# A projection made during the first layer norm and kept in DRAM until its gate, in a kernel of two transformer-like blocks

## The chip, the cores and the metric

One core of one Trainium2 chip runs the whole program; the other cores are idle. The metric is device time in microseconds (us) for one execution. The engines are TensorE (PE in the profile, its weight loads PEld), VectorE (DVE), ScalarE (ACT), GpSimd (POOL) and SyncE (SP, which here only issues transfers). Each has its own queue of instructions and works it off in order; semaphores tie the queues together.

## The reference, cut to what matters

Two blocks work on 1024 tokens of width 1024 in fp32. The first begins with a layer norm of the input and ends with a gate that adds a projection of a second input, p (1024 tokens, 256 features):

```python
x = layer_norm(x, ln_emb_g, ln_emb_b)
z = x @ w_in[i]
xs, gs, cq, ckv, kr, gm = jnp.split(z, IN_SPLIT_POINTS, axis=-1)
ys = s5_branch(xs, ...) * jax.nn.silu(gs)
ym = mla_branch(cq, ckv, kr, cos, sin, ...) * jax.nn.silu(gm)
mix = jnp.concatenate([ys, ym], axis=-1) @ w_out[i]
u = DEEPNORM_ALPHA * x + mix
ple = jax.nn.sigmoid(u @ w_pg[i]) * (p[i] @ w_pp[i])
x = layer_norm(u + ple, ln_g[i], ln_b[i])
```

p @ w_pp depends on nothing but inputs. The second block (two attentions, gates, a feed-forward part of width 2816) is not touched by the change.

## The kernel before, in words

All activations lie transposed: features on the 128 partitions, 1024 tokens along the free dimension. SBUF is divided by hand into 50 pages of 1024 fp32 columns (`page`, `pages`), which are used again and again for other things; weights pass through a ring of four pages (`ring`), filled by SyncE in a fixed order of blocks. `B_UKV`, `B_UQ`, `B_GLU`, `B_PP`, `B_WOUT` and so on number these blocks; block b goes to ring page b % 4, once the block that was there is used. The order of the work on each engine is the order in which the program is written for it, and every dependency is a semaphore.

A code matmul with fp32 operands shows as two records in the trace. A "tile" is 128 output features by 1024 tokens, over two PSUM banks of 512 columns (`two(b)` is banks b and b+1); a "half" is one bank.

**The start.** ScalarE issues the loads of the input (`xT`, four transfers of 1 MB into `XN`), then the constants. `norm_pe`, `norm_act` and `norm_dve` share the first layer norm, called `ln_emb`:

- TensorE sums the eight feature tiles of `XN` with a matrix of ones as they land (`sum_tiles`, L738), VectorE copies the mean out of PSUM (L903), TensorE spreads it to all partitions in banks 4 to 7 (`spread_tiles`, L745, read as `SPREAD`).
- VectorE subtracts it tile by tile (L906), ScalarE squares each tile into one of two buffers (`TEMPS_1`, L880), TensorE sums the squares (L738).
- ScalarE takes the root (L882), VectorE the reciprocal (L911), TensorE spreads it (L745).
- VectorE scales each tile (L898), ScalarE applies gain and bias (L892), and TensorE begins the first of 16 tiles of z = x @ w_in (`tile`, L2616), slice by slice as the tiles become ready. ScalarE copies these tiles out (L1527).

Meanwhile SyncE has waited for the last input (`landed3`) before it loads the first blocks of weights, and GpSimd prepares columns of the second block's modulation from them (`ada_sum`, L1300 to L1306: four additions or products per block).

**The end of the attention.** After the last head (L336 turns the probabilities, L348 multiplies by the values, L317 turns the output, VectorE gates it in L365) TensorE projects p: p was loaded by GpSimd into two pages of the attention's buffers (`PT_IN`, L1356), w_pp by SyncE as ring blocks `B_PP`. Eight tiles alternate between banks 0/1 and 2/3, ScalarE copies each into `PP` (L1615) and rounds one gated head in between (L1617), VectorE makes its low part (L2216). Then comes the output projection (`split_with_ada`, `products`, L2651), which needs each weight block in a high and a low part: GpSimd's `split` makes them (L1390, L1395), one block per tile, with an `ada_sum` in between. The projection of p is used in the gate, after the second projection `w_pg`, on VectorE.

## Time and profile before

| | |
|---|---|
| time before, median of 3 runs | 2281.03 us (2280.39 to 2282.52) |
| span of the profiled execution | 2278.5 us |
| what lies between the span and the median | 2.5 us |
| TensorE busy | 2194.5 us, 96% of the span |
| VectorE, GpSimd, ScalarE busy | 1154.4, 1192.3, 754.5 us |
| DMA over the span | mean 82 GB/s |

The device time of the profiled execution is not given apart from its span; the span starts with the first instruction and ends with the last, and the median of the timed runs is 2.5 us above it. "Busy" counts instructions that compute. The chain that ended last is followed back from the last instruction: what is on it sets the time. The granted clock (PEclk) is a share of TensorE's full clock of 2.4 GHz; its lower level, 1.2 GHz, shows as 0.50.

### The profile page before, as it was taken

Reading aid. Unit: us, or ns where it says so; the run is one execution under the profiler, and the core shown is the slowest. Engines: PE = TensorE matmul, PEld = TensorE weight load, DVE = VectorE, ACT = ScalarE, POOL = GpSimd, SP = SyncE. Lnnn points to the kernel's source line nnn. Section 1 sums busy time; section 2 is a strip of 40 time slices with the busy share of each in tenths; the row PEclk is TensorE's granted clock in tenths of the full one; section 3 lists DMA queues with packets and bytes.
Section 4 is the critical chain, followed back from the end, with each engine's and each line's share of the span. In section 5 each row is a group of like instructions: output and inputs, shape, how many; then the busy total and the mean of one; then the engine's idle time right before and its main releaser. Section 6 shows DMA issues by size and latency. Waiting matters only on the chain.

```text
span 2278.5 us, 27616 instructions
## 1 busy us (share of the span) xinstructions
PE 2194.5 (96%) x10944; PEld 1609.4 (71%) x10944; DVE 1154.4 (51%) x1473; ACT 754.5 (33%) x1161; POOL 1192.3 (52%) x809
## 2 busy tenths in 40 slices
PE   6999999999999899999999999998999999999998
PEld 2454464676886687568866788876788888888886
DVE  6950844551186611550036724775966666652434
ACT  4121042332112511650036343135555555531211
POOL 2533510204787265435656765365688888844442
PEclk8999999999999999999999999999999999999999
DMA  3336232001223422101211235233122222154111
GB/s 134 111 74 104 84 85 70 4 19 47 92 84 98 143 65 84 34 10 37 89 25 51 83 111 194 87 144 130 47 62 82 83 82 84 64 182 157 47 37 74
DMA packets 62590, 187.73 MB, mean 82 GB/s; under 512 B 14903, under 2 KB 17255, under 8 KB 62415
## 3 DMA queue, kind: packets, MB, share of 16 engines
q1 hardware_dynamic: 50688, 143.30, 19.6%
q10 hardware_dynamic: 8688, 32.26, 3.8%
q0 software_dynamic: 3088, 10.43, 2.4%
q8 instruction: 87, 1.43, 0.3%
q14 instruction: 39, 0.32, 0.0%
HBM read 150.15 MB, written 33.59 MB: 81 GB/s over the span
## 4 chain that ended last, share of the span: by engine, by line
PE 89%; DVE 5%; ACT 3%; issue 2%; POOL 1%; DMA 1%; ACTq 0%; DVEq 0%
PE ps L3005 21%; PE ps L2651 16%; PE ps L2616 14%; PE ps L3124 10%; PE ps L2929 4%; PE ps L3038 3%; PE ps L325 3%; PE ps L3076 2%; PE ps L493 1%; PE ps L481 1%; PE ps L348 1%; PE ps L2731 1%; PE ps L607 1%; PE ps L618 1%; PE ps L630 1%
## 5 line engine op out<-in xcount | busy, mean ns | idle before, releaser
L1390 POOL TENSOR_TENSOR w_parts<-front,sb_zero 128x1024 fp32r<-128x1024 f32 x69 | 139.0, 2014 | 300.8 <-PE ps L3124 117.7
L3124 PE MATMUL ps<-ffn_parts,w_parts 128*128 128x512 f32 x1008 | 230.3, 389 | 1.5 <-DVE front L2577 1.5
L1463 POOL TENSOR_TENSOR up_parts<-front,up_parts 128x512 fp32r<-128x512 f32 x120 | 194.5, 1629 | 69.5 <-ACT up_parts L1736 69.5
L2616 PE MATMUL ps<-front 128*128 128x512 f32 x512 | 225.5, 599 | 2.7 <-ACT front L892 2.7
L1395 POOL TENSOR_TENSOR w_parts<-front,w_parts 128x1024 fp32r<-128x1024 f32 x75 | 207.6, 2769 | 22.5 <-ACT w_parts L1891 7.5
L3124 PEld LDWEIGHTS ps<-ffn_parts,w_parts 128*128 128x128 f32 x1008 | 189.0, 188 | 41.7 <-issue 2.6
L1300 POOL TENSOR_TENSOR front<-front,sb_csilu 128x1024 f32<-128x1024 f32 x48 | 104.3, 2172 | 210.5 <-DMA front<-w_ada 210.5
L3005 PE MATMUL ps<-t_high,up_parts 128*128 128x512 f32 x640 | 204.8, 391 | 4.9 <-ACT back L1743 4.9
L2651 PE MATMUL ps<-h_high,w_parts 128*128 128x512 f32 x672 | 187.6, 394 | 0.6 <-PE ps L2929 0.6
L2616 PEld LDWEIGHTS ps<-front 128*128 128x128 f32 x512 | 96.5, 191 | 118.6 <-issue 118.1
L3005 PE MATMUL ps<-h_high,up_parts 128*128 128x512 f32 x480 | 154.5, 389 | 1.5 <-DVE back L2345 1.5
L1983 DVE TENSOR_TENSOR back<-back 128x1024 f32<-128x1024 f32 (+11 forms) x63 | 96.3, 1529 | 97.6 <-ACT back L1559 62.0
L3005 PEld LDWEIGHTS ps<-t_high,up_parts 128*128 128x128 f32 x640 | 121.0, 189 | 30.9 <-issue 5.7
L2651 PEld LDWEIGHTS ps<-h_high,w_parts 128*128 128x128 f32 x672 | 124.0, 188 | 25.8 <-issue 1.4
L2527 DVE TENSOR_TENSOR ffn_parts<-back,ffn_parts 128x1024 fp32r<-128x1024 f32 x44 | 70.0, 1599 | 129.4 <-ACT ffn_parts L1861 129.3
L1304 POOL TENSOR_TENSOR front<-front 128x512 f32<-128x512 f32 x96 | 123.7, 1289 | 7.5
L3005 PE MATMUL ps<-t_low,up_parts 128*128 128x512 f32 x320 | 125.2, 391 | 0.0
L2345 DVE TENSOR_TENSOR back<-ps,back 128x512 f32<-128x512 f32 x78 | 53.7, 688 | 113.3 <-PE ps L3005 82.8
L3005 PEld LDWEIGHTS ps<-h_high,up_parts 128*128 128x128 f32 x480 | 90.1, 188 | 20.5 <-issue 1.9
L2651 PE MATMUL ps<-h_low,w_parts 128*128 128x512 f32 x336 | 103.8, 390 | 0.0
L1861 ACT ACTIVATE ffn_parts<-back 128x1024 fp32r<-128x1024 f32 x44 | 46.3, 1060 | 158.9 <-PE ps L3124 158.9
L2616 PE MATMUL ps<-back,front 128*128 128x512 f32 x208 | 91.1, 595 | 2.8 <-ACT back L1598 1.2
(399 smaller groups left out, 4510.6 us busy)
## 6 DMA issues: line engine op xcount, KB each, us to landing
front<-w_ada SPq DMA_DIRECT2D x48, 512.0 KB, 3.6
front<-w_up SPq DMA_DIRECT2D x44, 512.0 KB, 4.4
front<-w_down SPq DMA_DIRECT2D x22, 512.0 KB, 3.6
front<-w_in SPq DMA_DIRECT2D x16, 512.0 KB, 3.6
front<-w_out SPq DMA_DIRECT2D x16, 512.0 KB, 4.7
residual<-back ACTq DMA_DIRECT2D x2, 4096.0 KB, 15.6
front<-w_gates SPq DMA_DIRECT2D x16, 512.0 KB, 4.0
gates<-back SPq DMA_DIRECT2D x16, 512.0 KB, 3.2
```

The costliest lines, as they stand in the source:

```text
L1300: pool.tensor_tensor(rows, rows, csilu[:].unsqueeze(2).to_broadcast((P, FT, P)), ALU.mult)\
L1304: pool.tensor_tensor(x[:, 0:w], x[:, 0:w], x[:, w:2 * w], ALU.add).then_inc(S("ada_step"), 1)
L1390: pool.tensor_tensor(high, raw, zero[:, 0:1].to_broadcast((P, PAGE)), ALU.add)\
L1395: pool.tensor_tensor(low, raw, high.bitcast(F32), ALU.subtract).then_inc(S("w_split"), 1)
L1463: pool.tensor_tensor(parts[:, BANK:], src, parts[:, 0:BANK].bitcast(F32), ALU.subtract)\
L1983: link(dve.tensor_tensor(o, a, b, op))
L2527: dve.tensor_tensor(AR[4 + kk % 4], act_at(kk), AR[kk % 4].bitcast(F32), ALU.subtract)\
L2616: mm = pe.matmul(ps[:, bank + nt, :], ring[:, slot, at + k * step:at + k * step + P], rhs(k0 + k)[:, nt * BANK:(nt + 1) * BANK], start=sta ...
L2651: mm = pe.matmul(ps[:, bank + nt, :], w_[:, k * P:(k + 1) * P], x_[k][:, nt * BANK:(nt + 1) * BANK], start=k == 0 and n == 0, stop=k == FT ...
L2929: mm = pe.matmul(ps[:, 2 * j + nt, :], WR[n % 2 + w_][:, at:at + P], x_[2 * b + k][:, nt * BANK:(nt + 1) * BANK], start=b == 0 and k == 0 ...
L3005: mm = pe.matmul(o, parts[:, at + k * P:at + (k + 1) * P], x, start=p in (1, 2, 5) and k == 0 and q == 0, stop=k == 3 and q == 2, skip_gro ...
L3124: mm = pe.matmul(ps[:, 2 * m + nt, :], parts[n % 2 + w_][:, at:at + P], half_of(AR[kk % 4 + x_], nt), start=k == 0 and q == 0, stop=k == N ...
```

## The change

The projection of p is taken from its place between attention and output projection and made during the first layer norm, in 16 halves (`pp_half`); it is stored to DRAM (`projected`) and loaded back by GpSimd when the pages of `PP` are free. Its inputs are loaded by SyncE ahead of and between the parts of the layer norm's input, which SyncE now loads too; ScalarE's loads of the constants move behind its first table loads. VectorE sums six of the eight input tiles (`X_SUM`), so TensorE needs three sums for the mean in place of eight. The layer norm of the start has functions of its own (`embed_pe`, `embed_act`, `embed_dve`). With `B_PP` gone, later blocks have numbers two lower. GpSimd starts the split of the first output weights on `mla_turned` (the last probabilities turned) and not on `mla_out` (the last output).

```diff
+        PT_FIRST, W_PP, PP_FIRST, X_SUM = pages(20, 2), pages(22, 2), pages(12, FT), page(27)
+        pp_dram = nc.dram_tensor("projected", (2, P, 4, SEQ), F32, kind="Internal").ap()
...
+        PP_BANK = (4, 5, 6, 7, 0, 1, 4, 5, 0, 1, 2, 0, 1, 2, 3, 2)
+        def pp_half(pe, s):
+            m, nt = divmod(s, 2)
+            for kt in range(2):
+                at = kt * BANK + m % 4 * P
+                mm = pe.matmul(ps[:, PP_BANK[s], :], W_PP[:, m // 4, at:at + P],
+                               PT_FIRST[:, kt, nt * BANK:(nt + 1) * BANK], start=kt == 0, stop=kt == 1)
+            mm.then_inc(S("pp_tile"), 1)
+        def embed_pe(pe):
+            pe.wait_ge(S("p_landed"), 32)
+            for s in range(8):
+                if s == 6:
+                    pe.wait_ge(S("pp_read_dve"), 1)
+                pp_half(pe, s)
+            pe.wait_ge(S("x_added"), 1)
+            sum_tiles(pe, 3, ones[:], X_SUM, True, False)
+            pe.wait_ge(S("landed3"), 16)
+            sum_tiles(pe, 3, ones[:], XN[:, 6, :], False, False)
+            sum_tiles(pe, 3, ones[:], XN[:, 7, :], False, True).then_inc(S("norm_mean"), 1)
+            pe.wait_ge(S("pp_free"), 3)
+            pe.wait_ge(S("norm_stat_read"), 1)
+            spread_tiles(pe, TEMPS_1[2][:, 0:256]).then_inc(S("norm_mean_spread"), 1)
+            pe.wait_ge(S("w_pp_landed"), 16)
+            pp_half(pe, 8)
+            pp_half(pe, 9)
+            for k in range(FT):
+                if k == 2:
+                    pp_half(pe, 10)
+                pe.wait_ge(S("norm_square"), k + 1)
+                sum_tiles(pe, 3, ones[:], TEMPS_1[k % 2], k == 0, k == FT - 1).then_inc(S("norm_square_used"), 1)
+            pe.wait_ge(S("pp_free"), 4)
+            pp_half(pe, 11)
+            pe.wait_ge(S("norm_rstd"), 1)
+            spread_tiles(pe, TEMPS_1[2][:, 256:512]).then_inc(S("norm_spread"), 1)
+            pp_half(pe, 12)
+            pe.wait_ge(S("pp_free"), 5)
+            pp_half(pe, 13)
+            pe.wait_ge(S("norm_std"), 1)
+            pp_half(pe, 14)
+            pe.wait_ge(S("pp_free"), 8)
+            pp_half(pe, 15)
...
+        def embed_act(act):
...
+            for m in range(1, 4):
+                projected(2 * m, 2, m)
+            act.wait_ge(S("pp_read_dve"), 1)
+            act.wait_ge(S("pp_free"), 3)
+            act.dma_start(pp_dram[0], PP_FIRST[:, 0:4, :]).then_inc(S("pp_out0"), 16)
...
+            projected(8, 2, 4)
+            act.wait_ge(S("norm_square_used"), FT)
+            act.activation(TEMPS_1[2][:, 256:512], ps[:, 3, 0:256], ACT.Sqrt, bias=eps[:, 0:1]).then_inc(S("norm_std"), 1)
+            projected(10, 1, 5)
+            projected(11, 1, 6)
+            late = {0: 12, 2: 13, 3: 14, 5: 15}
+            for k in range(FT):
+                act.wait_ge(S("norm_scaled"), k + 1)
+                act.activation(XN[:, k, :], XN[:, k, :], ACT.Identity, scale=V("ln_emb_g", k), bias=V("ln_emb_b", k))\
+                    .then_inc(S("norm_ready"), 1)
+                if k in late:
+                    projected(late[k], 1, 0)
+            act.wait_ge(S("pp_free"), 10)
+            act.dma_start(pp_dram[1], PP_FIRST[:, 4:8, :]).then_inc(S("pp_out1"), 16)
...
+        def embed_dve(dve, link):
+            dve.wait_ge(S("pp_tile"), 2)
+            dve.tensor_copy(PP_FIRST[:, 0, :], two(4)).then_inc(S("pp_read_dve"), 1)
+            for k in range(1, 6):
+                dve.wait_ge(S(f"landed{k // 2}"), 16)
+                ins = dve.tensor_tensor(X_SUM, XN[:, 0, :] if k == 1 else X_SUM, XN[:, k, :], ALU.add)
...
+            sp.dma_start(PT_FIRST, t["pT"].rearrange("(k p) t -> p k t", p=P)).then_inc(S("p_landed"), 16)
+            sp.dma_start(W_PP[:, 0, :], t["w_pp"][0]).then_inc(S("p_landed"), 16)
+            sp.dma_start(XN[:, 0:2, :], x_in[:, 0:2, :]).then_inc(S("landed0"), 16)
+            sp.dma_start(W_PP[:, 1, :], t["w_pp"][1]).then_inc(S("w_pp_landed"), 16)
+            for h in range(1, 4):
+                sp.dma_start(XN[:, 2 * h:2 * h + 2, :], x_in[:, 2 * h:2 * h + 2, :]).then_inc(S(f"landed{h}"), 16)
             sp.wait_ge(S("landed3"), 16)
...
-            for k in range(2):
-                pool.wait_ge(S("mla_turned"), 30 + k)
-                pool.dma_start(PT_IN[k], t["pT"][k * P:(k + 1) * P, :]).then_inc(S("p_landed"), 16)
-            pool.wait_ge(S("mla_out"), 32)
+            pool.wait_ge(S("mla_turned"), 32)
...
                 split(B_WOUT + 2 * j)
+                if j == 0:
+                    pool.dma_start(PP, pp_dram.rearrange("a p k t -> p a k t")).then_inc(S("pp_back"), 16)
                 ada_sum(16 + j)
...
-            for m in range(8):
-                act.wait_ge(S("pp_tile"), m + 1)
-                act.activation(PP[:, m, :], two(2 * (m % 2)), ACT.Copy).then_inc(S("pp_free"), 1)
-                if m % 2:
-                    act.activation(MH[4 + m // 2], GM[:, m // 2, :], ACT.Copy).then_inc(S("gm_high"), 1)
+            act.wait_ge(S("mla_out"), 32)
+            for h in range(MLA_HEADS):
+                act.activation(MH[4 + h], GM[:, h, :], ACT.Copy).then_inc(S("gm_high"), 1)
...
+            dve.wait_ge(S("pp_back"), 16)
...
+            embed_pe(pe)
             pe.wait_ge(S("act_step"), ACT_STEP["c_ready"])
+            pe.wait_ge(S("pp_free"), 7)
...
-            for m in range(8):
-                block_landed(B_PP + m // 4)
-                if m == 1:
-                    pe.wait_ge(S("mla_scores_read"), 32 + MLA_HEADS)
-                elif m >= 2:
-                    pe.wait_ge(S("pp_free"), m - 1)
-                mm = tile(2 * (m % 2), (B_PP + m // 4) % RING, lambda k: PT_IN[k], kts=2,
-                          at=(m % 4) * P, step=BANK)
-                mm.then_inc(S("pp_tile"), 1)
```

The order of instructions shows the two places. On TensorE, the first layer norm, from the first matmul of the program to the last of the layer norm (L738 sums, L745 spreads, L997 is a matmul of `pp_half`; a code matmul is counted once here):

```order
-L738 MATMUL ps<-front,sb_ones 32x256 x32
+L997 MATMUL ps<-back 128x512 x16
+L738 MATMUL ps<-back,sb_ones 32x256 x4
+L738 MATMUL ps<-front,sb_ones 32x256 x8
 L745 MATMUL ps<-back,sb_pick 128x256 x4
-L738 MATMUL ps<-back,sb_ones 32x256 x32
+L997 MATMUL ps<-back 128x512 x4
+L738 MATMUL ps<-back,sb_ones 32x256 x8
+L997 MATMUL ps<-back 128x512 x2
+L738 MATMUL ps<-back,sb_ones 32x256 x24
+L997 MATMUL ps<-back 128x512 x2
 L745 MATMUL ps<-back,sb_pick 128x256 x4
```

The 32 matmuls of the mean's sums become 12, and 16 of the projection stand ahead of them; eight more (halves 8 to 11) stand among the sums of squares, and eight (halves 12 to 15) behind the last spread, ahead of the first z tile.

On GpSimd, the end of the attention. Before, two loads of p, then the first split (L1390, L1395), the additions for the modulation, the second split:

```order
L1356 DMA back<-pT 128x1024 [waits mla_turned] x2
L1390 TENSOR_TENSOR w_parts_0_57<-front,sb_zero 128x1024 [waits w_landed3,mla_out]
L1395 TENSOR_TENSOR w_parts_2_59<-front,w_parts_0_57 128x1024 [waits w_high]
L1300 TENSOR_TENSOR front<-front,sb_csilu 128x1024 [waits w_landed0]
L1304 TENSOR_TENSOR front<-front 128x512 [waits ada_step]
```

And with the change, where L1498 and L1503 are the split and L1411 begins the additions:

```order
L1498 TENSOR_TENSOR w_parts_0_57<-front,sb_zero 128x1024 [waits w_landed1,mla_turned]
L1503 TENSOR_TENSOR w_parts_2_59<-front,w_parts_0_57 128x1024 [waits w_high]
L1519 DMA back<-projected 128x2x4096
L1411 TENSOR_TENSOR front<-front,sb_csilu 128x1024 [waits w_landed2]
L1415 TENSOR_TENSOR front<-front 128x512 [waits ada_step]
```

The loads of p are gone, the first split waits for an earlier semaphore, and the load of the stored projection (4 MB) is issued between it and the additions.

## Rows read from the trace of the kernel before

**Rows 1.** The page's chain of work that ended last, shares by engine.
```profile
PE 89%; DVE 5%; ACT 3%; issue 2%; POOL 1%; DMA 1%; ACTq 0%; DVEq 0%
```

**Rows 2.** The same chain in order of time, first 120 us: start, us, what.
```profile
3.18 12.37 DMA front<-xT
...
15.59 1.87 PE ps L738 x16
...
19.27 9.15 DVE front L906 x8
...
30.76 1.76 DVE back L911
...
32.57 1.08 PE ps L745 x8
...
36.31 22.49 PE ps L2616 x48
...
58.91 13.84 PE ps L2616 x32
```

**Rows 3.** Busy time by stretch; last columns granted clock, DMA share, GB/s.
```profile
core 0: us, PE busy (x) PEld busy (x) DVE busy (x) ACT busy (x) POOL busy (x), PEclk, DMA share, GB/s
...
6.00:15.50 9.50, 4.94 (x48) 1.70 (x48) 1.31 (x8) 6.30 (x10) 0.00 (x0) 1.00 1.00 399
15.50:19.20 3.70, 3.08 (x24) 1.10 (x24) 0.43 (x1) 0.00 (x0) 0.00 (x0) 0.53 0.68 223
19.20:30.30 11.10, 6.86 (x64) 1.44 (x64) 9.14 (x8) 8.47 (x9) 8.68 (x8) 0.69 0.30 118
...
36.30:39.70 3.40, 3.39 (x4) 1.49 (x5) 3.40 (x4) 3.40 (x4) 0.00 (x0) 0.51 0.00 0
39.70:51.90 12.20, 12.20 (x30) 5.45 (x29) 10.73 (x44) 4.39 (x4) 0.00 (x0) 1.00 0.00 1
```

**Rows 4.** DMA traffic from 0 to 20 us, in 40 slices.
```profile
GB/s 0 0 0 32 89 256 82 254 377 410 393 410 402 418 410 410 434 410 442 410 418 426 402 442 410 410 393 381 406 393 161 25 25 131 197 319 410 361 418 434
```

**Rows 5.** Timeline of ScalarE at the start: start, us, engine, line, what.
```profile
1.66 2.24 ACTq L1498 DMA_DIRECT2D front<-xT  x4
...
12.74 0.20 ACT L1517 ACTIVATE sb_stat<-sb_eps 128x1 f32<-128x1 f32 x1
...
20.52 8.98 ACT L880 ACTIVATE back<-front 128x1024 f32<-128x1024 f32 x8 [7.58 <-DVE front L906]
...
34.93 9.16 ACT L892 ACTIVATE front<-front,sb_vec 128x1024 f32<-128x1024 f32 x8 [4.20 <-DVE front L898]
```

**Rows 6.** The chain that ended last, from 508 to 562 us.
```profile
512.59 3.36 PE ps L348 x30
...
517.54 13.75 PE ps L2616 x32
...
545.85 16.16 PE ps L2651 x70
```

**Rows 7.** Timeline from 516 us: GpSimd, ScalarE and VectorE.
```profile
516.03 1.89 POOL L1390 TENSOR_TENSOR w_parts<-front,sb_zero 128x1024 fp32r<-128x1024 f32 x1 [6.14 <-PE ps L348]
...
518.00 2.35 POOL L1395 TENSOR_TENSOR w_parts<-front,w_parts 128x1024 fp32r<-128x1024 f32 x1
520.30 1.90 POOL L1300 TENSOR_TENSOR front<-front,sb_csilu 128x1024 f32<-128x1024 f32 x1
...
524.43 0.46 POOL L1306 TENSOR_TENSOR front<-front 128x128 f32<-128x128 f32 x1
...
525.37 1.05 ACT L1617 ACTIVATE mix_high<-back 128x1024 fp32r<-128x1024 f32 x1
526.45 1.22 DVE L2216 TENSOR_TENSOR mix_low<-back,mix_high 128x1024 fp32r<-128x1024 f32 x1 [7.64 <-ACT mix_high L1617]
```

**Rows 8.** Timeline: GpSimd issues a 2 MB load; SyncE fills a ring slot.
```profile
339.75 0.78 POOL L1343 DMA_DIRECT2D back<-ssm_out_by_feature  x1 [11.43 <-DMA ssm_out_by_feature<-back]
...
396.48 0.33 SPq L1134 DMA_DIRECT2D front<-w_ada  x1
```

More of the change, by code:

```diff
@@ new lines, in embed_act, with projected @@
+        def embed_act(act):
+            def projected(s, n, done):
+                m, nt = divmod(s, 2)
+                act.wait_ge(S("pp_tile"), s + n)
+                act.activation(PP_FIRST[:, m, nt * BANK:(nt + n) * BANK],
+                               ps[:, PP_BANK[s]:PP_BANK[s] + n, :].rearrange("p a b -> p (a b)"),
+                               ACT.Copy).then_inc(S("pp_free"), 1)
+            for m in range(1, 4):
[4 more added lines that the diff above has]
+            for k in range(FT):
+                act.wait_ge(S("norm_centred"), k + 1)
+                if k >= 2:
+                    act.wait_ge(S("norm_square_used"), k - 1)
+                act.activation(TEMPS_1[k % 2], XN[:, k, :], ACT.Square).then_inc(S("norm_square"), 1)
+            projected(8, 2, 4)
[4 more added lines that the diff above has]
+            late = {0: 12, 2: 13, 3: 14, 5: 15}
+            for k in range(FT):
+                act.wait_ge(S("norm_scaled"), k + 1)
[5 more added lines that the diff above has]
+            act.dma_start(pp_dram[1], PP_FIRST[:, 4:8, :]).then_inc(S("pp_out1"), 16)
@@ new lines, in embed_dve @@
+        def embed_dve(dve, link):
[4 more added lines that the diff above has]
+                ins = dve.tensor_tensor(X_SUM, XN[:, 0, :] if k == 1 else X_SUM, XN[:, k, :], ALU.add)
+                if k < 5:
+                    link(ins)
+            ins.then_inc(S("x_added"), 1)
+            dve.wait_ge(S("norm_mean"), 1)
+            dve.tensor_copy(TEMPS_1[2][:, 0:256], ps[:, 3, 0:256]).then_inc(S("norm_stat_read"), 1)
+            dve.wait_ge(S("norm_mean_spread"), 1)
+            for k in range(FT):
+                dve.tensor_tensor(quarters(XN[:, k, :]), quarters(XN[:, k, :]), SPREAD, ALU.subtract)\
+                    .then_inc(S("norm_centred"), 1)
+            dve.wait_ge(S("norm_std"), 1)
+            dve.reciprocal(TEMPS_1[2][:, 256:512], TEMPS_1[2][:, 256:512]).then_inc(S("norm_rstd"), 1)
+            dve.wait_ge(S("norm_spread"), 1)
+            for k in range(FT):
+                dve.wait_ge(S("norm_centred"), k + 1)
+                dve.tensor_tensor(quarters(XN[:, k, :]), quarters(XN[:, k, :]), SPREAD, ALU.mult)\
+                    .then_inc(S("norm_scaled"), 1)
@@ L991, in program @@
         BLOCKS_WIN = 32
-        B_UKV, B_UQ, B_GLU, B_PP = 32, 33, 35, 37
-        B_WOUT = 39
+        B_UKV, B_UQ, B_GLU = 32, 33, 35
+        B_WOUT = 37
         B_WPG = B_WOUT + 16
@@ L1158, in _ @@
             loads(B_GLU, B_GLU, [tile_of(t["w_glu"], m) for m in range(2)])
-            loads(B_PP, B_PP, [tile_of(t["w_pp"], m) for m in range(2)])
             def slot_free(b):
@@ L1496, in _ @@
             act.dma_start(vec[:], t["vec"]).then_inc(S("vec_landed"), 16)
-            for h in range(4):
-                act.dma_start(XN[:, 2 * h:2 * h + 2, :], t["xT"].rearrange("(k p) t -> p k t", p=P)
-                              [:, 2 * h:2 * h + 2, :]).then_inc(S(f"landed{h}"), 16)
-            act.dma_start(ident[:], t["ident"]).then_inc(S("consts_landed"), 16)
-            act.dma_start(BC, t["ssm"][:, 3 * PAIRS:].rearrange("p (i q c) -> p i q c", i=4, q=PAIRS))\
-                .then_inc(S("consts_landed"), 16)
-            act.dma_start(dsk[0:GC, :], t["dsk"]).then_inc(S("consts_landed"), 16)
-            act.dma_start(rope_c[:], t["rope_c"]).then_inc(S("consts_landed"), 16)
             act.wait_ge(S("vec_landed"), 32)
@@ L2821, in split_with_ada @@
                         pe.wait_ge(S(free), m - 1)
+                    elif before:
+                        pe.wait_ge(S(before), 7 + m)
                     else:
-                        pe.wait_ge(S(before), 7 + m)
+                        pe.wait_ge(S("mla_scores_read"), 32 + MLA_HEADS - 1 + m)
                     products(2 * (m % 2), *w_parts_1(base + 2 * m), high, low, "w_used" if m else None,
```

24 lines of the change are left out of this document (12 added, 12 removed).

## The prediction

> **What bounds the kernel now.** I read the chain of the work that ended last first: 89% of the span is TensorE [rows 1], so an edit counts for what it takes from or adds to TensorE's path, and other engines count where TensorE waits. Then I read the chain at the two places that the change touches. At the start it is not TensorE: the input lands until 15.55, and from there copy, spread, subtraction, squares, root, reciprocal and spread pass from engine to engine until the first input-projection tile starts at 36.31 [rows 2]. In the stretches 6.0 to 15.5, 15.5 to 19.2 and 19.2 to 30.3 TensorE is busy 4.9, 3.1 and 6.9 us, most of it with short sums [rows 3]. From 36.31 on it works without a break. At 517.54 the chain shows the projection of p: 32 matmul records in 13.75 us, 32 more behind them, and the output projection starts at 545.85 [rows 6]. Nothing hides it: the chain holds TensorE alone there.
>
> **What is removed: 28.3 us.** With the 8 tiles gone, the output projection can start where they started: 545.85 - 517.54 = 28.3, if its inputs are there. The weights' parts come from GpSimd in 1.89 + 2.35 us [rows 7]. Before, it starts them at 516.03, on the last attention output; now on the last transpose of scores, and the matmuls behind that transpose start at 512.59 [rows 6]. Parts ready at 512.6 + 4.3 = 516.9, 0.6 ahead of TensorE. The first four input slices were split long before. The last four need the last head: ScalarE rounds one in 1.05, VectorE subtracts in 1.22 [rows 7]. VectorE's last gating product ends near 518.8 (it starts when the transposes before 517.54 end, and takes about as long as that subtraction), so the slices stand at 521.1, then one each 1.2. TensorE wants the fifth half a tile later: 24 of 72 records in 16.16 for 70 [rows 6] are 5.5 us, so 523.1. No wait.
>
> The second tile is where the lost cover shows. GpSimd must issue the 4 MB load of the projection, do the four additions for the modulation (520.30 to 524.89, 4.6) and split again (4.3). The issue isn't in the trace: the nearest row, half as large, took 0.78 [rows 8]; below it the floor is nothing, above it twice, 1.6. I take 1.0. So 516.9 + 1.0 + 4.6 + 4.3 = 526.8, and TensorE comes at 517.54 + 11.1 = 528.6: 1.8 to spare. The raw blocks are there: the ring slots that w_pp held are freed to w_out and w_ada, and the fourth is filled at 396.48 [rows 8]. Later tiles cost GpSimd 8.9 against TensorE's 11.1. The 4 MB load lies beside weight loads; at 0.41 MB/us it is over some 12 us after 518, and the next block is wanted at 531. VectorE wants the result 150 us later. The 8 copies from PSUM on ScalarE (1.02 each) were off the path.
>
> **What is added at the start.** Times in the new schedule are primed.
>
> First the loads. The input came at 377 to 442 GB/s once it flowed [rows 4]; I use 0.415 MB/us. Landing at 15.55 with 4.19 MB of input and 0.17 ahead puts the last byte near 13.6, so completion costs 1.9. SyncE can issue about 0.9 us earlier than ScalarE did, whose four input loads begin at 1.66 [rows 5]. Ahead of the projection lie 0.17 + 1.05 (p) + 0.52 (half of w_pp) MB: 4.2 us from 2.3, plus 1.8: TensorE starts at 8.2'. All 6.3 MB, and the constants (0.6 MB), which ScalarE now issues after its table loads (the first instruction behind them was at 12.74 [rows 5], now some 2 earlier) and which thus compete, make the last input land at about 21.0'.
>
> Then 8 halves, 32 records. A tile of 32 records costs 13.84 at the upper clock [rows 2, 3]. TensorE comes from idle, and in the same case at 36.31 the granted clock was 0.51 for 3.4 us (the 1.2 GHz level, against 1.00 at 2.4) [rows 3]; half of that is lost, 1.7. So 8.2 + 13.8 + 1.7 = 23.7', later than the input: **TensorE is what the mean waits for**, not the load. Bounds: no low stretch 22.0'; one of twice the length 25.4'. VectorE's five additions (1.22 each, like the subtraction in [rows 7]) follow the landings and end about 21.0'; its copy of tile 0 goes before them. Hidden; without the cover of TensorE's 8 halves they would cost 1.2. Three sums instead of eight remain: before, the last two took 1.87 at the low clock [rows 2]; three at the high one are 1.4 to 1.6: 25.3'. Copy and spread took 1.8, from 17.46 to 19.27 [rows 2], the spread at the low clock; at the high one it should be 0.5 less: the mean is spread at 26.6', before 19.2. **+7.4.**
>
> Variance. The first square ends 2.4 after the spread before (VectorE subtracts in 1.14 [rows 2], ScalarE squares in 1.12 [rows 5]). Now halves 8 and 9 take 3.5 first and half 10 another 1.7 before the third sum. Both square buffers wait for those sums. Followed through, the last sum ends 11.85 after the spread instead of 11.0. A 1.02 copy of tile 4 stands ahead of the root on ScalarE, partly beside the last sum: +0.5. Half 11 (1.7) fits beside root and reciprocal (the latter 1.76 [rows 2]). The spread, 1.08 before, should be 0.4 quicker at the high clock. **+0.9**: reciprocal spread at 42.0', before 33.65.
>
> Halves 12 to 15. They stand between the spread and the first z tile. 12, 13 and 14 end 5.2 after it; 15 waits until ScalarE has read 13, behind three applications of gain and bias (1.15 each [rows 5]) and one copy: 5.9, so it ends at 7.7. The first z tile starts 7.8 after the spread, before 2.7: +5.1. But before it ran its first 3.4 us at the low clock, which the halves now do away with: -1.7. Its inputs are ahead of it. **+3.4.**
>
> Sum at the start: 7.4 + 0.9 + 3.4 = 11.7. VectorE's tables are later by only 8.3, and GpSimd's and ScalarE's later work hangs on TensorE or on those tables, so everything up to 517 shifts by 11.7 and no more. The two stores of the projection go to queues that nothing waits on before the first z tile's copy, 10 us after the first store should be over.
>
> **Sum.** 28.3 - 11.7 = 16.6 us less. The profiled execution has a span of 2278.5, so 2261.9; the median of the runs is 2281.03, 2.5 above the span, and I take the difference over to it: **2264.4**.
>
> **Rivals.**
> 1. The forecast, 0.74.
> 2. A wait in front of the output projection takes the place of the matmuls. For it: GpSimd had 28.3 us of cover and has 1.8 to spare now, with an issue of unknown length. Against it: all its other durations are rows. If the split started as late as before (516.03) TensorE would wait 2.8 at the first tile; if the 4 MB issue took 5 us, 2.2 at the second. Gain 13.8: 2267.2. Chance 0.10.
> 3. The loads bound the mean. Should the two queues get 0.33 MB/us together, the input lands at 25' and the mean shifts by 1.5 to 3: 2266 to 2268. For it: DMA is at 1.00 already from 6 to 15.5 [rows 3]. Chance 0.05.
> 4. The clock falls back in the gaps of the layer norm. Before, it stood at 0.53 from 15.5 to 19.2 with TensorE busy 3.1 of 3.7 us, and at 0.69 on average until 30.3 [rows 3]. Halves 8 to 10 would then cost 5 more, 12 to 15 6, the z tile its 1.7 again: 12.7 less gain, 2277.1. Against it: those were sums on 32 columns with waits between; now dense matmuls fill the gaps. Chance 0.07, the full price; part of it lies in my range. This is also what the Trainium skill says (TensorE: Matmul & The Clock Gate, HAM oscillation): pauses between bursts send the array back to half clock. By that rule the trace agrees at 36.31.
> 5. Slower: the clock stays at the low level through the whole projection. The first 8 halves would end at 35.7', 12 later, and with rival 4's 12.7 and 2 for sums and spreads: 26.7 against 16.6, 2291. It decides from 33 us of low clock beyond the 3.4 assumed, at half a us each. Against it: at 36.31 the same kind of matmul had the full clock after 3.4. Chance 0.04.
>
> **Range and chances.** Low: no low stretch at the start (-1.7), loads 1.5 earlier, spread and sums 1 less, and some for the z tiles: 2259.5. High: a low stretch of twice the length (+1.7), a second one (+1.7), rival 2 (+2.8), rounded: 2271.5. It holds cases 1 to 3 and a little of 4, 0.87. What a measurement can tell from no change is 0.2%, 4.6 us. Faster: cases 1 to 3 and part of 4, 0.92; same: the rest of 4, 0.04; slower 0.04.
>
> **What would show it.** First projection matmul near 8.2', the 8 halves over near 23.7', after the last input landed; the mean's sums right behind them. Granted clock 1.00 from some 12' to the first z tile, which starts near 49.8' and takes 13.8. The output projection's first matmul within 1 us of the last transposes of attention, at 529'; no wait over 1 us at its second tile. Wrong would be: sums that wait for the input after the halves, clock near 0.5 around 30', GpSimd's split the last to end before the second tile, or a longer pause anywhere between 52 and 517 than before.

## The result, and the profile after

The changed kernel takes 2266.12 us (median of 4 runs, 2264.39 to 2267.58); the kernel before, on the same chip, 2280.71 (4 runs, 2278.19 to 2282.52). The ratio is 0.9936, 95% interval 0.9924 to 0.9948: 14.6 us less, where 16.6 were forecast (2264.4). The profiled execution has a span of 2262.4 us; it is the fastest of the four, 2264.39, and its span is 16.1 below that of the profile before. So times at fixed points of the two traces are compared below, and not the spans.

The page's chain by engine reads almost as before [rows 1]; it moves too little to say where the time went:

```profile
PE 89%; DVE 4%; ACT 3%; issue 2%; POOL 1%; DMA 0%; DVEq 0%; ACTq 0%; SPq 0%
```

The chain in order of time does. At the start (start, us, what), against [rows 2]:

```profile
1.25 6.15 DMA back<-w_pp
...
7.54 16.65 PE ps L997 x32
24.19 1.48 PE ps L738 x24
...
26.27 0.71 PE ps L745 x8
26.98 3.63 PE ps L997 x8
...
39.42 1.76 DVE back L1086
...
41.23 0.76 PE ps L745 x8
...
47.79 1.98 PE ps L997 x4
```

The first eight halves (L997) run from 7.54 to 24.19, and the mean's three sums (L738) stand right behind them: TensorE is what the mean waits for. The mean is spread at 26.98, the reciprocal at 41.99, and the first z tile starts at 49.77. Before, these three stood at 19.27, 33.65 and 36.31.

The halves began at the low clock. The profile's granted-clock column (the third number from the end) says 1.00 from the start:

```profile
7.50:13.30 5.80, 5.76 (x7) 2.45 (x8) 1.31 (x8) 5.02 (x9) 0.00 (x0) 1.00 1.03 412
```

But the weight loads give it away (timeline of TensorE's weight loads):

```profile
11.09 0.34 PEld L997 LDWEIGHTS ps<-back 128*128 128x128 f32 x1 [0.52 <-issue]
11.94 0.34 PEld L997 LDWEIGHTS ps<-back 128*128 128x128 f32 x1 [0.52 <-issue]
12.80 0.27 PEld L997 LDWEIGHTS ps<-back 128*128 128x128 f32 x1 [0.52 <-issue]
13.30 0.19 PEld L997 LDWEIGHTS ps<-back 128*128 128x128 f32 x1 [0.24 <-issue]
13.73 0.19 PEld L997 LDWEIGHTS ps<-back 128*128 128x128 f32 x1 [0.24 <-issue]
```

Up to 12.80 they follow each other every 0.85 us, and from 13.30 every 0.43. In the trace before, the same kind of loads stood 0.85 apart where the granted clock was 0.51 [rows 3] and 0.43 apart where it was 1.00. So this is the 1.2 GHz level for 5.7 us, then 2.4 GHz, which stays until the z tile. Half of 5.7 is lost, 2.9.

On the way to the output projection little else moved. The last transposes stood at 511.53 before and stand at 523.13 now: 11.6 later, where 11.7 were forecast. Behind them is what was not forecast (the chain again, 523 to 559 us, against [rows 6]):

```profile
523.13 1.08 PE ps L338 x8
...
524.27 1.90 POOL w_parts L1498
...
526.24 2.35 POOL w_parts L1503
528.59 0.66 POOL back L1519
...
529.27 1.92 POOL front L1411
...
531.26 1.31 POOL front L1415
...
532.64 1.61 POOL front L1415
...
534.32 1.32 POOL front L1417
535.64 2.84 POOL w_parts L1498
...
538.55 3.26 POOL w_parts L1503
541.81 0.04 issue
541.85 5.78 PE ps L2758 x24
547.63 0.12 PE ps L2736 x2
```

The chain leaves TensorE and runs over GpSimd until 541.81; the waits of TensorE in this stretch (total, times, longest) are, for the output projection:

```profile
PE ps L2758 <- DVE mix_low L2322: 0.9, 1, 0.9
PE ps L2758 <- POOL w_parts L1503: 0.6, 1, 0.6
```

GpSimd's instructions are longer than the same ones are elsewhere. The addition over 128x128 takes 1.32 here and 0.46 in [rows 7], rounding a block (the first half of its split) 2.88 against 1.89, subtracting (the second half) 3.25 against 2.35. VectorE's low parts, 1.22 in [rows 7], take 8.03 for four (VectorE's timeline, the four asked for in windows that end later and later, so that each row holds one more):

```profile
531.53 2.12 DVE L2322 TENSOR_TENSOR mix_low<-back,mix_high 128x1024 fp32r<-128x1024 f32 x1 [1.12 <-ACT mix_high L1722]
531.53 3.79 DVE L2322 TENSOR_TENSOR mix_low<-back,mix_high 128x1024 fp32r<-128x1024 f32 x2 [1.12 <-ACT mix_high L1722]
531.53 5.20 DVE L2322 TENSOR_TENSOR mix_low<-back,mix_high 128x1024 fp32r<-128x1024 f32 x3 [1.12 <-ACT mix_high L1722]
531.53 8.03 DVE L2322 TENSOR_TENSOR mix_low<-back,mix_high 128x1024 fp32r<-128x1024 f32 x4 [1.12 <-ACT mix_high L1722]
```

They end at 533.65, 535.32, 536.73 and 539.56. Set beside these the ends of GpSimd's instructions in the chain above (start plus length): 532.57, 534.25, 535.64, 538.48, 541.81. Each of VectorE's ends comes 1.07 to 1.09 after one of GpSimd's, and each of GpSimd's then 0.60, 0.32, 1.75 and 2.25 after VectorE's, which is its length without company (0.75, 0.46, 1.89, 2.35) less 0.10 to 0.15. The two engines take turns, instruction by instruction: whichever starts while the other works waits until it is done. That costs GpSimd 3.6 us and VectorE 3.4 (without company the four take 4.63, experiment 7).

It isn't any work of VectorE that does this. In the first layer norm of the same kernel GpSimd's additions run beside VectorE's subtractions, which read one operand from PSUM (`ps`), and both keep the lengths that they have alone:

```profile
27.04 9.14 DVE L1083 TENSOR_TENSOR front<-front,ps 128x1024 f32<-128x1024 f32 x8 [0.92 <-PE ps L745]
29.68 0.46 POOL L1417 TENSOR_TENSOR front<-front 128x128 f32<-128x128 f32 x1
```

The low parts read both operands from SBUF.

The two waits above, 1.5 us, and some 0.4 that the tiles lose besides, are the stall. The first column for the modulation (L2736 now, L2629 before; it stands behind 72 records of the output projection in both) is at 547.63; before at 562.46. So 14.83 are gained there: 28.3 - 11.6 = 16.7, less 1.9. From that column to the end no kernel here changes anything but what GpSimd does beside the first tiles; it took 1716.0 us before and 1714.8 now, and between 1714.8 and 1717.9 in the profiles of this document (experiment 7 apart, whose stall lies behind the column). So single spans and single times differ by up to 3 us for reasons that lie behind the change.

### The profile page after: what moved, and what is told of

The parts are those of the page before. It is cut to its first block, busy times and chain, and to the rows that moved or that the text cites. A ratio compares the mean times of both kernels' runs of the same rounds, so it can differ in the third digit from the quotient of the medians.

```text
span 2262.4 us, 27546 instructions
## 1 busy us (share of the span) xinstructions
PE 2186.6 (97%) x10904; PEld 1606.9 (71%) x10904; DVE 1163.2 (51%) x1479; ACT 753.0 (33%) x1163; POOL 1190.1 (53%) x808
## 4 chain that ended last, share of the span: by engine, by line
PE 89%; DVE 4%; ACT 3%; issue 2%; POOL 1%; DMA 0%; DVEq 0%; ACTq 0%; SPq 0%
PE ps L3100 21%; PE ps L2758 16%; PE ps L2723 13%; PE ps L3219 11%; PE ps L3024 4%; PE ps L3133 3%; PE ps L327 3%; PE ps L3171 2%; PE ps L493 1%; PE ps L481 1%; PE ps L350 1%; PE ps L997 1%; PE ps L2838 1%; PE ps L618 1%; PE ps L630 1%
## 5 line engine op out<-in xcount | busy, mean ns | idle before, releaser
L1498 POOL TENSOR_TENSOR w_parts<-front,sb_zero 128x1024 fp32r<-128x1024 f32 x69 | 140.5, 2037 | 374.5 <-PE ps L3219 117.7
L1503 POOL TENSOR_TENSOR w_parts<-front,w_parts 128x1024 fp32r<-128x1024 f32 x75 | 208.8, 2784 | 22.9 <-ACT w_parts L1996 7.5
L1411 POOL TENSOR_TENSOR front<-front,sb_csilu 128x1024 f32<-128x1024 f32 x48 | 102.7, 2140 | 216.9 <-DMA front<-w_ada 216.9
L2088 DVE TENSOR_TENSOR back<-back 128x1024 f32<-128x1024 f32 (+11 forms) x63 | 90.6, 1437 | 96.8 <-ACT back L1666 62.0
L1415 POOL TENSOR_TENSOR front<-front 128x512 f32<-128x512 f32 x96 | 117.7, 1226 | 7.5
L1848 ACT ACTIVATE back<-ps 128x512 f32<-128x512 f32 x98 | 58.6, 598 | 105.8 <-PE ps L3100 99.7
```

The costliest lines, as they stand in the source:

```text
L1411: pool.tensor_tensor(rows, rows, csilu[:].unsqueeze(2).to_broadcast((P, FT, P)), ALU.mult)\
L1415: pool.tensor_tensor(x[:, 0:w], x[:, 0:w], x[:, w:2 * w], ALU.add).then_inc(S("ada_step"), 1)
L1498: pool.tensor_tensor(high, raw, zero[:, 0:1].to_broadcast((P, PAGE)), ALU.add)\
L1503: pool.tensor_tensor(low, raw, high.bitcast(F32), ALU.subtract).then_inc(S("w_split"), 1)
L2088: link(dve.tensor_tensor(o, a, b, op))
```

## The experiments

Each experiment was timed beside the kernel before, whose medians there were 2280.16 to 2280.74 us (2280.71 for the change). A difference between an experiment and the change thus carries some tenths of a us of its own, and the column's place in the traces is given beside it.

**1. The projection taken out altogether.** The gate gets the input in place of the projection (its output isn't the reference's), the layer norm is the old one, GpSimd's early split and 4 MB load stay.

```diff
-            embed_pe(pe)
+            norm_pe(pe, "ln_emb", FT, lambda k: XN[:, k, :], ones[:], True, TEMPS_1,
+                    lambda k: pe.wait_ge(S(f"landed{k // 2}"), 16))
...
-                    pool.dma_start(PP, pp_dram.rearrange("a p k t -> p a k t")).then_inc(S("pp_back"), 16)
+                    pool.dma_start(PP, t["xT"].rearrange("(k p) t -> p k t", p=P)).then_inc(S("pp_back"), 16)
```

> The end of the change alone: the projection of p is left out everywhere (the gate gets the input in its place, loaded by the same kind of 4 MB transfer, so the output is another), the first layer norm is as before the change, the split starts early. Theory: the removed matmuls are worth 28.3 us less the waits that the trace after shows at the output projection, 26.5 us, whatever happens at the start: about 2254.2 against 2280.7, and the first z tile starts at 36.3 again. Difference to the changed kernel: the whole price of the start, 11.6. Rival: the start costs less than the traces say because later stages absorb part of it (tables on VectorE, transfers), then this kernel stands at 2256 or above.

Measured: 2254.44 us (2253.42 to 2256.52), ratio 0.9889 (0.9873 to 0.9906). The z tile starts at 35.43. VectorE's four low parts take 8.22 and the waits are 1.08 and 0.58, as with the projection. So what is added at the start costs 2266.12 - 2254.44 = 11.7 us, the forecast's number; taken each against its own kernel before it is 11.5, and at the last transposes (510.94 against 523.13) 12.2, because here the input landed 0.7 earlier than in the profile before (14.84 against 15.55), which no run explains. And the stall at the output projection comes from what lies around it there, not from the projection's new place.

**2. The mean's sums all on TensorE.** VectorE's five additions go; TensorE sums eight slices instead of three.

```diff
-            pe.wait_ge(S("x_added"), 1)
-            sum_tiles(pe, 3, ones[:], X_SUM, True, False)
+            for k in range(6):
+                pe.wait_ge(S(f"landed{k // 2}"), 16)
+                sum_tiles(pe, 3, ones[:], XN[:, k, :], k == 0, False)
```

> The changed kernel without its second part: TensorE sums all eight tiles of the input for the mean, VectorE's running sum is gone. Theory: TensorE is what the mean waits for, so five sums more of 8 records stand on the path, at 1.07 us for 16 records: 2.6 us more than the changed kernel, about 2268.7. Rival: the load binds, then the sums hide beside the landings and it costs nothing.

Measured: 2268.51 us (2267.70 to 2269.19), ratio 0.9949 (0.9932 to 0.9966). From its chain:

```profile
24.20 3.64 PE ps L738 x64
```

The sums take 3.64 instead of 1.48, the z tile starts at 51.94 instead of 49.77, and the time is 2.4 longer. TensorE binds the mean, and the running sum on VectorE is worth 2.2 to 2.4 of the gain: it is hidden on VectorE and would not be on TensorE.

**3. Warming TensorE.** Ten small matmuls of ones before p has landed.

```diff
+            for i in range(10):
+                pe.matmul(ps[:, 2, 0:P], ones[:], ones[:], start=True, stop=True)
             pe.wait_ge(S("p_landed"), 32)
```

> The changed kernel, with ten small matmuls of the ones matrix on TensorE between 2.9 us and the landing of p, their result unused. Theory: the first 8 halves took 16.65 us where 13.84 is the price at the high clock, because TensorE came from idle; with matmuls ahead of them the clock rises earlier, the 8 halves take 13.9 to 14.6, the mean's sums begin near 21.5 to 22 in place of 24.2 (the input has landed at 20.5), and everything shifts: 2.2 to 2.8 us less than the changed kernel, about 2263.6. Rival A: the load of the input binds the mean, then nothing or under 0.5 us is gained. Rival B: such matmuls don't raise the clock; the halves take 16.6 again and the time is as in the changed kernel.

Measured: 2263.99 us (2263.38 to 2264.67), ratio 0.9927 (0.9911 to 0.9944). Its chain:

```profile
7.59 14.00 PE ps L997 x32
```

14.00 instead of 16.65, the upper clock from the first half on, and the z tile at 47.17, 2.6 earlier; 2.1 in the times. So the low stretch was paid in full: the mean waits for nothing else that would have hidden it.

**4. Half of the projection.** The second 128 features of p are not added (the gate's input isn't the reference's).

```diff
-            for kt in range(2):
+            for kt in range(1):
...
-                               PT_FIRST[:, kt, nt * BANK:(nt + 1) * BANK], start=kt == 0, stop=kt == 1)
+                               PT_FIRST[:, kt, nt * BANK:(nt + 1) * BANK], start=True, stop=True)
```

> The changed kernel with half of the projection's matmuls left out (the second 128 features of p are not added), loads, copies and waits as they are. Theory: the first 8 halves end near 17.5 to 18 (from 7.5, low clock at first), before the last input at 20.5, so now the load binds: sums of the mean at 20.6 in place of 24.2. The squares' sums slip by nothing, the late halves end about 1 us earlier: first z tile near 43.8 in place of 49.8, span about 2256.5. Rival: if the load were already near binding, the mean would move by under 1 us and the z tile by under 3.

Measured: 2264.84 us, a single run, span 2262.9. The sums now wait for the input (`DMA front<-xT` in the chain until 20.84), as expected: the loads would bind next, some 3 us below TensorE. But the z tile starts at 45.69, not at 43.8, and the column for the modulation that follows its 48 records stands at 67.82, where 64.4 would be right (43.8 and 20.6 for the records at the upper clock). The busy time by stretch (busy of PE, PEld, DVE, ACT, POOL; granted clock; DMA share; GB/s), against [rows 3]:

```profile
16.60:20.80 4.20, 0.64 (x8) 0.16 (x8) 2.62 (x3) 1.02 (x1) 0.00 (x0) 1.00 1.09 434
20.80:24.20 3.40, 2.70 (x24) 1.03 (x24) 0.42 (x1) 0.00 (x0) 0.00 (x0) 0.58 1.01 434
24.20:28.00 3.80, 3.80 (x12) 1.25 (x12) 3.66 (x4) 2.11 (x2) 0.00 (x0) 0.50 0.95 389
44.40:48.50 4.10, 4.10 (x6) 1.83 (x7) 3.87 (x8) 4.10 (x5) 0.00 (x0) 0.60 0.00 0
```

TensorE worked 0.64 of 4.2 us ahead of 20.80, and then got 0.58 and 0.50 of the clock; it stood still for 3.07 us ahead of 44.40, and got 0.60. This is the forecast's rival 4. With the full projection it stayed away: there the granted clock is 1.00 from 24.2 to 49.7, with TensorE busy 22.2 of these 25.5 us. The total is no guide here: a single run lies within a range of some 2 to 3 us.

**5. The same with the gaps filled.** The half projection again (the gate's input isn't the reference's), 14 small matmuls of ones ahead of the mean's sums and 12 ahead of the last half.

```diff
+            for i in range(14):
+                pe.matmul(ps[:, 2, 0:P], ones[:], ones[:], start=True, stop=True)
             pe.wait_ge(S("x_added"), 1)
...
+            pe.wait_ge(S("pp_free"), 7)
+            for i in range(12):
+                pe.matmul(ps[:, 1, 0:P], ones[:], ones[:], start=True, stop=True)
             pe.wait_ge(S("pp_free"), 8)
```

> The second 128 features of p are again not added to the projection (so the gate's input is not the reference's), and TensorE gets 14 small matmuls of ones between the first eight halves and the mean's sums, and 12 before the last half. Theory (the run with half of the projection missed its 43.8 us because TensorE's clock fell in its idle time, twice): the mean's spread takes 0.7 us instead of 1.24, the four matmuls behind it 1.9 instead of 3.7, the first z tile begins at 43.0 to 44.0 us instead of 45.69 and takes 20.6 us instead of 22.13, so that its ada column comes at about 64.2 instead of 67.82. Rival (the chain through VectorE and ScalarE binds, whatever the clock): z tile at 45.7 us, with only the 1.5 us of its own slow start gained.

Measured: 2260.06 us, a single run, span 2258.1. The same stretches:

```profile
20.80:24.20 3.40, 2.68 (x27) 1.25 (x28) 1.26 (x2) 0.00 (x0) 0.00 (x0) 1.00 0.90 386
44.40:48.50 4.10, 4.10 (x10) 1.72 (x10) 3.70 (x12) 4.10 (x5) 0.00 (x0) 1.00 0.09 40
```

The clock is 1.00 in both, the four records behind the spread take 1.98 instead of 3.7, the z tile runs 20.60 instead of 22.13 for 48 records, and its column stands at 64.98, 2.8 earlier. The z tile itself starts at 44.38, 1.3 earlier than in experiment 4 and 0.4 above what was expected. The chain shows why: from 23.36 it runs over VectorE's subtractions (`DVE front L1088 x8`, 9.15 us), so what TensorE gains behind the spread is partly given back, as the rival had it. Of the 3.4 us that experiment 4 missed at its column, the clock was 2.8. The totals differ by 4.8, of which 2.0 lie behind the output projection's first tiles: the columns there stand 2.8 apart too (545.04 and 542.24). The Trainium skill says the same of pauses between bursts of matmuls, that TensorE falls back to its lower clock in them (TensorE: Matmul & The Clock Gate, HAM oscillation); the 0.58 and 0.60 here agree.

**6. The transfer back issued at the fourth block.** It takes the 4 MB from the stretch in which VectorE and GpSimd are slow.

```diff
-                if j == 0:
+                if j == 3:
                     pool.dma_start(PP, pp_dram.rearrange("a p k t -> p a k t")).then_inc(S("pp_back"), 16)
```

> The changed kernel with the 4 MB load of the stored projection issued three tiles later (after the split of the fourth block). In the changed kernel, between 531.3 and 541.8, VectorE's subtractions of the low parts took 2.0 us each in place of 1.22, GpSimd's additions 2.98 and 1.32 for 2.07 and 0.46, its split 2.88 and 3.25 for 1.89 and 2.35. Theory: VectorE and GpSimd slow each other when both work on SBUF operands at once, so all these stay as long; only the issue (0.72) is gone, TensorE's wait for the second block's parts (0.59) goes, its wait for the last low part (0.9) stays: 0.6 us less. Rival: the transfer of 4 MB slows them; then VectorE is back at 1.22, GpSimd at its former times, both waits go, 1.5 to 1.9 us less.

Measured: 2266.70 us, a single run, span 2264.7. GpSimd's instructions are as long as before (1.32, 2.87, 3.25), VectorE's four 7.29 instead of 8.03, the waits 0.17 and 0.59, and the second tile starts 0.74 earlier (the column 0.8, at 546.84); that the time is 0.6 above the change's is within the range of a single run. Without the 0.7 of the issue GpSimd's and VectorE's turns fall otherwise; the transfer isn't what makes them slow.

**7. GpSimd waits for VectorE.** The second block is split only when the four low parts stand; the transfer runs beside them.

```diff
+            split(B_WOUT)
+            pool.dma_start(PP, pp_dram.rearrange("a p k t -> p a k t")).then_inc(S("pp_back"), 16)
+            pool.wait_ge(S("gm_split"), 4)
+            split(B_WOUT + 2)
             for j in range(8):
-                split(B_WOUT + 2 * j)
-                if j == 0:
-                    pool.dma_start(PP, pp_dram.rearrange("a p k t -> p a k t")).then_inc(S("pp_back"), 16)
+                if j > 1:
+                    split(B_WOUT + 2 * j)
```

> The changed kernel, where GpSimd, after the first split and the issue of the 4 MB load, waits until VectorE has made its four low parts, then splits the second block, then does the additions. The 4 MB transfer stays where it was. Theory (VectorE and GpSimd slow each other): VectorE's four subtractions take 1.22 each, the split 1.89 and 2.35, TensorE's wait at the last low part goes, at the second tile it waits some 0.5 us for the split; 1 us less in all. Rival (the transfer slows both): subtractions stay near 2.0 each, the split starts only at 539.6, TensorE waits 3 us or more at the second tile.

Measured: 2269.86 us, a single run, span 2267.8. VectorE's timeline:

```profile
531.36 4.63 DVE L2325 TENSOR_TENSOR mix_low<-back,mix_high 128x1024 fp32r<-128x1024 f32 x4 [1.13 <-ACT mix_high L1725]
```

4.63 for the four (1.22 for one), with the 4 MB beside them, and the split behind it takes 1.88 and 2.38. So it is GpSimd's company, not the transfer and not the matmuls (TensorE works through the whole stretch here too), that makes the low parts slow. The first column for the modulation stands at 546.20, 1.4 earlier than in the change, as expected. The time was not won, though. The additions and the third split came that much later, and the third tile now waited for them (chain):

```profile
549.57 1.86 POOL w_parts L1498
...
551.50 2.37 POOL w_parts L1503
...
553.91 7.36 PE ps L2761 x24
```

The wait at the third tile is 2.02, and behind it the clock falls (same columns as in experiment 4):

```profile
553.90:557.50 3.60, 3.59 (x11) 2.90 (x12) 0.00 (x0) 0.34 (x1) 3.44 (x3) 0.68 0.00 0
```

So the 24 records behind the wait take 7.36 where the 48 of a tile take 11.01 in the change, 1.9 more than their share. The wait costs nearly twice its length, and the next column stands at 561.27, 2.5 later than in the change.

**8. The split of the first block as late as before.**

```diff
-            pool.wait_ge(S("mla_turned"), 32)
+            pool.wait_ge(S("mla_out"), 32)
```

> The changed kernel with one part undone: GpSimd starts the first split on the last attention output, as before the change, 3.4 us later (527.6 for 524.3 in the trace). Theory: the parts stand at 531.9, TensorE waits 2.8 us before the output projection; the second block's parts come 3.4 later as well, so from the second tile on everything is 3.4 us later than in the changed kernel, about 2269.5. Rival: GpSimd catches up, since VectorE's subtractions then overlap less of its work: 2.5 to 3 us.

Measured: 2269.39 us (2268.18 to 2270.24), ratio 0.9951 (0.9935 to 0.9966), 3.3 more than the change. TensorE waits 2.86 for w_parts, until 532.11, and here too the clock falls behind the wait:

```profile
532.10:536.00 3.90, 3.89 (x11) 3.08 (x12) 3.90 (x3) 2.35 (x3) 3.80 (x3) 0.59 0.84 277
```

The 72 records from 532.11 to the column take 18.21, against 16.37 in experiment 10, where TensorE doesn't wait: 1.8 more. So the late split costs 2.86 + 1.8 = 4.7, in place of the 1.9 that the change loses here (TensorE comes so late that GpSimd's and VectorE's turns no longer hold it up): 2.8 more, 2.7 at the column (550.33), 3.3 in the times. Waiting for the last transposes instead of the last output is a needed part of the change.

**9. Warm, both splits first, transfer later.**

```diff
+            for i in range(10):
+                pe.matmul(ps[:, 2, 0:P], ones[:], ones[:], start=True, stop=True)
             pe.wait_ge(S("p_landed"), 32)
...
+            split(B_WOUT)
             for j in range(8):
-                split(B_WOUT + 2 * j)
                 if j == 0:
+                    split(B_WOUT + 2)
+                elif j > 1:
+                    split(B_WOUT + 2 * j)
+                if j == 3:
                     pool.dma_start(PP, pp_dram.rearrange("a p k t -> p a k t")).then_inc(S("pp_back"), 16)
```

> The changed kernel with the small matmuls ahead of the projection, with the second block split ahead of the additions for the modulation, and with the 4 MB load issued at the fourth block. Theory: 2.2 to 2.8 us from the clock, 0.6 from the wait for the second block's parts (the wait for the last low part, 0.9, stays or grows a little, as the split is as heavy on VectorE as the additions): 3 us less than the changed kernel, about 2263.0. Rival: one of the gains is given back, 2264.5 or above.

Measured: 2263.86 us (2263.23 to 2266.49), ratio 0.9930 (0.9917 to 0.9944), no better than the warm start alone (2263.99). Both splits are over at 530.34, but the additions of the modulation, now beside the low parts, take turns with them: VectorE's four take 9.23, and TensorE waits 0.94 and 0.58 for them.

**10. The same, and GpSimd pauses before the additions.** The edit is shown against the change, the small matmuls left out.

```diff
+            split(B_WOUT)
+            split(B_WOUT + 2)
+            pool.wait_ge(S("gm_split"), 4)
             for j in range(8):
-                split(B_WOUT + 2 * j)
-                if j == 0:
+                if j > 1:
+                    split(B_WOUT + 2 * j)
+                if j == 3:
                     pool.dma_start(PP, pp_dram.rearrange("a p k t -> p a k t")).then_inc(S("pp_back"), 16)
```

> Ten small matmuls of ones before p lands, and on GpSimd both first weight blocks split, then a wait for the fourth low part of VectorE, and only then the two ada additions; the transfer back is issued at the fourth block. Theory (VectorE and GpSimd slow each other while both work on operands in SBUF, and the additions came too early): the low parts take about 1.22 us each as soon as the second split is done (530.3 us), both waits for mix_low (0.94 and 0.58 us in the kernel that had the additions right behind the splits) go, the second tile begins at about 536.7 instead of 538.2 and the time is 2262.3 us. The additions are over by 543 us and the third split by 547, ahead of their use at 543.9 and 549. Rival 1 (the slow low parts have another cause, such as the matmuls beside them): VectorE 9.2 us for four, waits as before, 2263.9 us. Rival 2 (the additions or the third split come too late, as in the run in which GpSimd waited for all low parts): the waits stand before the second tile's ada column or the third tile, 2264 to 2267 us.

Measured: 2261.89 us (2261.41 to 2263.12), ratio 0.9918 (0.9904 to 0.9931). VectorE's and TensorE's rows (timeline; the low parts' line with min, median and max in ns; chain):

```profile
529.13 5.89 DVE L2328 TENSOR_TENSOR mix_low<-back,mix_high 128x1024 fp32r<-128x1024 f32 x4 [1.13 <-ACT mix_high L1728]
L2328 DVE TENSOR_TENSOR mix_low<-back,mix_high x4: 1209/1211/2485, 529.1 to 533.8; 128x1024 fp32r<-128x1024 f32 x4
526.74 16.37 PE ps L2764 x72
```

The first low part starts at 529.13 beside GpSimd's second subtraction, which ends at 530.53, and takes 2.485: again until 1.08 after GpSimd's end. The other three take 1.21. TensorE goes through both tiles without a wait, and the first column for the modulation stands at 543.11, 4.5 earlier than in the change and 2.2 earlier than in experiment 9. GpSimd's additions and its third split, over at 544.3 and 548.6, are now in time. This kernel takes 4.2 us less than the change; by the trace it is 4.5, of which 2.4 come from the warm start (the last transposes stand at 520.73) and 2.1 from the turns.

## Why the prediction was right, and where it was not

The sign, the place and the size of both sides held, with a stall of 1.9 us that the forecast had at nothing. Step by step:

- **Removed, 28.3.** TensorE's 8 tiles are gone, and the output projection starts right behind the last transposes. Right.
- **First projection matmul 8.2'.** 7.54, the loads were 0.7 quicker.
- **The low stretch, 3.4 us for 1.7.** It was 5.7 for 2.9. The row it was taken from [rows 3] showed TensorE after short sums, not after standing still since the start; whether that is the reason for the longer stretch no run shows. Warming gave back 2.6 (experiment 3). Of the error of 1.2 the earlier start made good 0.7: the halves ended at 24.19 for 23.7'.
- **TensorE, not the load, is what the mean waits for; VectorE's additions are hidden.** Experiment 2 shows that TensorE binds, and experiment 4 that the load is some 3 us below and that VectorE's sum stands before it (19.61, the input 20.84).
- **Mean 26.6', reciprocal 42.0', z tile 49.8', sum 11.7.** 26.98, 41.99, 49.77, and 11.7 by experiment 1 (11.6 in the trace at 523.13). The last two agree to 0.03, and that is partly luck: the mean came 0.4 late, and the variance took 0.4 less than forecast (15.0 for 15.4). The -1.7 for the z tile's start holds: no low stretch there.
- **Splitting at the last transposes** is worth 3.3 in the times (experiment 8). Rival 2 put a late split at a wait of 2.8. The wait was 2.86, but the rival left out the clock, which fell behind it: 1.8 more.
- **The issue of the 4 MB load, 1.0.** 0.72.
- **The 2.5 us between span and median, taken over.** In the profiled execution of the change the span is 2.0 below its own time (2262.4 and 2264.39). The forecast of the span, 2261.9, was missed by only 0.5; that is luck in part, since this execution is the fastest of the four.
- **"Then one each 1.2", "No wait", "1.8 to spare".** Here it failed. Each duration came from a row in which the other engine did nothing, and the two were added up as if VectorE and GpSimd could work side by side. They take turns in this stretch: the low parts took 2.0 each and GpSimd's four instructions 3.6 longer. Without that GpSimd would have been done at 541.81 - 3.6 = 538.2, ahead of TensorE, which came near 540.4 (its first tile ended at 541.26, 0.9 of it a wait). So the sum of the durations was fair, and the rule that they may be summed engine by engine wrong. It cost 1.9, nearly all of the 2.0 that the gain came short. One of the forecast's own signs of being wrong came up with it: GpSimd's split was the last to end before the second tile (541.81, TensorE at 541.85), though neither wait reached 1 us. Rival 2 named the place, but the wait's cause there was a late split or a long issue, and neither happened.

The trace of before had it. Near 65 us GpSimd's additions over 128x512 (timeline of the kernel before) ran beside VectorE's long products, 128x2048 with both operands in SBUF:

```profile
64.94 5.93 POOL L1304 TENSOR_TENSOR front<-front 128x512 f32<-128x512 f32 x2
```

5.93 for two that take 2.1 elsewhere (22.58 to 24.67 in the same trace, beside subtractions that read PSUM). The Trainium skill states the rule (SBUF — State Buffer, Who interferes with whom): a VectorE instruction with both inputs in SBUF contends with a GpSimd instruction that reads SBUF, and whichever issues first holds the shared ports to its end while the other blocks. The ends 1.07 to 1.09 us after one another agree with it, and so does experiment 7, where the low parts without GpSimd's company took 1.22 each.

## What to carry to other kernels

Where VectorE and GpSimd both stand between two stretches of a third engine, and their instructions read two operands from SBUF, don't take the later end of two sums: add the two engines' instructions up in one queue, and look for a stretch of the trace in which the two overlap. Letting one pause can pay (experiment 10), but only while the work that it puts off has slack (experiment 7). A wait of TensorE may cost more than its length: behind 2.02 and 2.86 us the clock fell, and 1.9 and 1.8 us more went (experiments 7 and 8). Work put into the pauses of the start is cheaper than its length (28.3 us of matmuls cost 11.7 here): most of that is time in which TensorE would have waited, and some 1.9 came from the clock, which it keeps up for the first z tile (that tile starts 13.5 later than before, the last transposes 11.6). A few small matmuls of ones ahead of it gave 2.6 more.

## What the runs showed of the hardware that was not expected

- VectorE's and GpSimd's two-input instructions on SBUF excluded each other for their whole length, in turns: 1.22 us became 1.4 to 2.9, and 0.46 became 1.32. VectorE's subtractions with one operand in PSUM did not disturb GpSimd (0.46 beside them).
- A 4 MB transfer into SBUF beside the same instructions cost them nothing (1.22 each, experiment 7).
- From a standing start the 1.2 GHz level lasted 5.7 us of dense matmuls, against 3.4 after short sums [rows 3]; the profile's granted clock says 1.00 there, and only the spacing of the weight loads (0.85, then 0.43) shows it.
- Behind a pause of TensorE of 3.07 us the granted clock was 0.60 over the next 4.1 us, and behind a stretch with 0.64 us of work in 4.2 it was 0.58 and 0.50 over the next 3.4 and 3.8; with small matmuls in them it stayed at 1.00 (experiments 4 and 5). Waits of 2.86 and of 2.02 us were followed by 0.59 over 3.9 us and 0.68 over 3.6 (experiments 8 and 7).
